# Two-part products in the FFN and column tiles: one wide product for the high weights, halves added at eviction

## What is computed

```python
for l in range(2):                                   # first block
    ...
    hf = rms_norm(x, ffn_norm[l]) @ w_up[l]          # 1024 -> 2 x 2816
    gate, val = hf[..., :2816], hf[..., 2816:]
    gate = depthwise_conv(gate, conv_w[l], conv_b[l])   # 3 taps over the tokens, and a bias
    x = x + (gelu(gate) * val) @ w_down[l]
for l in range(2):                                   # second block
    proj = x @ w_in[l]                               # column part: 10 tiles of 128 channels
    ...
    q = h @ peer_w_q[l]                              # 1024 -> 2048: 16 tiles of 128 channels
    ...
```

## Time and profile before

| | |
|---|---|
| median of three runs | 2944.22 us (2942.88 to 2944.81) |
| the profiled execution | 2944.41 us, its span 2942.6 us |
| instructions in the span | 57193 |
| TensorE busy | 2712.1 us (92%), 17384 matmuls |
| weight loads | 2423.4 us (82%), 17384 |
| VectorE busy | 2088.4 us (71%) |
| ScalarE busy | 1481.8 us (50%) |
| GpSimd busy | 220.9 us (8%) |
| mean granted TensorE clock | 0.961 of full speed |

### The profile page before, as it was taken

One profiled execution on the slowest core, in us unless ns is written; L12 is line 12 of the kernel. 1 busy time (PEld: TensorE's weight loads), 2 busy tenths in 40 slices (PEclk: granted clock), 3 DMA queues, 4 the chain that ended last, 5 costly groups with the idle time before them and its releaser, 6 DMA issues. The chain is left out here.

```text
span 2942.6 us, 57193 instructions
## 1 busy us (share of the span) xinstructions
PE 2712.1 (92%) x17384; PEld 2423.4 (82%) x17384; DVE 2088.4 (71%) x4674; ACT 1481.8 (50%) x2884; POOL 220.9 (8%) x168
## 2 busy tenths in 40 slices
PE   7989989989985899899999999976999899999997
PEld 6759988679874899899988888855999899988886
DVE  5757767567667658977767777676569777777776
ACT  5545555545432445456655555524454466555554
POOL 0000000000020034400000000200144100000000
PEclk9999999999985999999999999977999999999999
DMA  5225553246540557655567777612577555577775
GB/s 190 85 65 172 184 191 101 72 131 184 184 166 1 162 179 229 188 159 174 174 204 233 232 232 233 206 57 79 154 229 215 158 173 176 171 233 234 234 233 180
DMA packets 194020, 504.57 MB, mean 171 GB/s; under 512 B 22528, under 2 KB 88320, under 8 KB 192512
## 3 DMA queue, kind: packets, MB, share of 16 engines
q1 hardware_dynamic: 193920, 503.33, 55.2%
HBM read 468.64 MB, written 34.60 MB: 171 GB/s over the span
## 5 line engine op out<-in xcount | busy, mean ns | idle before, releaser
L182 DVE TENSOR_TENSOR w_lo<-w_raw,w_hi 128x512 fp32r<-128x512 f32 (+2 forms) x1432 | 973.3, 684 | 341.8 <-ACT w_hi L173 321.4
L173 ACT ACTIVATE w_hi<-w_raw 128x512 fp32r<-128x512 f32 (+2 forms) x1592 | 927.1, 621 | 267.4 <-PE banks_right L217 136.8
L215 PE MATMUL up_up<-hT_hi,w_hi 128*128 128x256 f32 x2048 | 594.4, 290 | 26.8 <-DVE w_lo L182 20.7
L217 PE MATMUL up_up<-hT_hi,w_lo 128*128 128x256 f32 x2048 | 581.6, 284 | 0.0
L216 PE MATMUL up_up<-hT_lo,w_hi 128*128 128x256 f32 x2048 | 581.1, 284 | 0.0
L215 PEld LDWEIGHTS up_up<-hT_hi,w_hi 128*128 128x128 f32 x2048 | 394.8, 193 | 31.2 <-DVE w_lo L182 24.0
L227 PE MATMUL banks_left<-w_hi,expert_hi 128*128 128x512 f32 x1024 | 407.6, 398 | 7.8 <-DVE w_lo L182 7.8
L228 PE MATMUL banks_left<-w_lo,expert_hi 128*128 128x512 f32 x1024 | 406.9, 397 | 0.0
L229 PE MATMUL banks_left<-w_hi,expert_lo 128*128 128x512 f32 x1024 | 406.9, 397 | 0.0
L216 PEld LDWEIGHTS up_up<-hT_lo,w_hi 128*128 128x128 f32 x2048 | 394.4, 193 | 0.0
L217 PEld LDWEIGHTS up_up<-hT_hi,w_lo 128*128 128x128 f32 x2048 | 393.7, 192 | 0.0
(11 more groups left out here) (366 smaller groups left out, 4162.3 us busy)
## 6 DMA issues: line engine op xcount, KB each, us to landing
w_raw<-in_peer_u_c SPq DMA_DIRECT2D x256, 512.0 KB, 3.6
w_raw<-in_peer_v SPq DMA_DIRECT2D x256, 512.0 KB, 3.6
w_raw<-in_w_up_c SPq DMA_DIRECT2D x88, 512.0 KB, 3.7
expert_gelu_held<-expert_gelu SPq DMA_DIRECT2D x256, 128.0 KB, 1.8
expert_back<-expert_gelu_held SPq DMA_DIRECT2D x256, 128.0 KB, 3.4
w_raw<-in_w_down SPq DMA_DIRECT2D x44, 512.0 KB, 4.3
w_raw<-in_w_in_r SPq DMA_DIRECT2D x40, 512.0 KB, 3.6
w_raw<-in_w_in_c SPq DMA_DIRECT2D x32, 512.0 KB, 3.7
```

Of the source, the lines that this page charges most:

```text
L173: self.nc.scalar.activation(self.w_hi[:, k % SLOTS, 0:width], self.raw_half(k, width), ACT.Copy).then_inc(self.sem("w_hi_done"), 1)
L182: self.nc.vector.tensor_tensor(self.w_lo[:, k % SLOTS, 0:width], self.raw_half(k, width), self.w_hi[:, k % SLOTS, 0:width].bitcast(F32), A ...
L215: self.nc.tensor.matmul(bank, hi, self.hT_hi[:, c, :], start=(c == 0), stop=False)
L217: last = self.nc.tensor.matmul(bank, lo, self.hT_hi[:, c, :], start=False, stop=(c == DC - 1))
```

## The change

hT_hi and hT_lo become the two halves of one tile, hT, in which the 256 values of the low part follow the 256 of the high part in each chunk. A new `wide_col_half` multiplies w_hi with both in one matmul of 512 columns, which fills a whole PSUM bank: the first 256 values are products with hT_hi, the others with hT_lo. A second matmul adds w_lo with hT_hi to the first 256. The two halves of the bank are added at eviction by VectorE, with a `tensor_reduce` over pairs of values that lie 256 apart. `project` and `gated_loop` use it; the first block's own column tiles and the experts' up products keep `col_half`. In `project` the reduction takes the place of the copy. In `gated_loop` there are two reductions per tile (gate and value) into a new SBUF tile, then a wait for them, and the convolution and the product read that tile instead of PSUM.

```diff
-        self.hT_hi = self.sb("hT_hi", [P, DC, SEQ], F32R)
-        self.hT_lo = self.sb("hT_lo", [P, DC, SEQ], F32R)
+        self.hT = self.sb("hT_hi_lo", [P, DC, 2, SEQ], F32R)
+        self.hT_hi, self.hT_lo = self.hT[:, :, 0, :], self.hT[:, :, 1, :]
...
+    def wide_col_half(self, pe, k, bank, rep=0, entry=None):
+
+        pe.wait_ge(self.sem("w_lo_done"), k + 1 + 2 * SLOTS * rep)
+        for j in range(4):
+            c = 4 * (k % 2) + j
+            if entry is not None:
+                entry.chunk_ready(pe, c)
+            hi = self.w_hi[:, k % SLOTS, j * P:(j + 1) * P]
+            lo = self.w_lo[:, k % SLOTS, j * P:(j + 1) * P]
+            self.nc.tensor.matmul(bank, hi, self.hT[:, c].rearrange("p a n -> p (a n)"), start=(c == 0), stop=False)
+            last = self.nc.tensor.matmul(bank[:, 0:SEQ], lo, self.hT_hi[:, c, :], start=False, stop=(c == DC - 1))
+        last.then_inc(self.sem("w_used"), 1)
...
-                    nc.vector.tensor_copy(cols_dst[:, j, :], col[:, j % 2, 0:SEQ]).then_inc(col_free, 1)
+                    nc.vector.tensor_reduce(cols_dst[:, j, :], col[:, j % 2].rearrange('p (a n) -> p n a', a=2), AX.X,
+                                            ALU.add).then_inc(col_free, 1)
...
-                    K.col_half(pe, k0 + 2 * j + h, col[:, j % 2, 0:SEQ], entry=entry if j == 0 else None)
+                    K.wide_col_half(pe, k0 + 2 * j + h, col[:, j % 2], entry=entry if j == 0 else None)
...
+    both = K.sb(f"{name}_up", [P, 2, n_up, SEQ], F32, ctx)
...
-                nc.scalar.activation(ge[:, b, :], act_in(up, b), ACT.Gelu).then_inc(gelu_done, 1)
+                act.wait_ge(pre_done, j + 1 + unroll * n)
+                nc.scalar.activation(ge[:, b, :], act_in(both, b), ACT.Gelu).then_inc(gelu_done, 1)
...
             def pre(j, n):
-                if gate_dve is not None:
-
-                    dve.wait_ge(used, up_used(j) + 2 * SLOTS * rounds * n)
-                    gate_dve(dve, up, j % 2, j + unroll * n, pre_done)
+                dve.wait_ge(used, up_used(j) + 2 * SLOTS * rounds * n)
+                for q in range(n_up):
+                    nc.vector.tensor_reduce(both[:, j % 2, q, :], up[:, j % 2, q].rearrange("p (a n) -> p n a", a=2), AX.X,
+                                            ALU.add).then_inc(sum_done, 1)
+                dve.wait_ge(sum_done, n_up * (j + unroll * n) + n_up)
+                gate_dve(dve, both, j % 2, j + unroll * n, pre_done)
...
-                nc.vector.tensor_tensor(ac[:, b, :], ge[:, b, :], mult_by(up, b, j + unroll * n),
+                nc.vector.tensor_tensor(ac[:, b, :], ge[:, b, :], mult_by(both, b, j + unroll * n),
...
-                        K.col_half(pe, first + 2 * q + h, up[:, j % 2, q, 0:SEQ], rep=rounds * n,
-                                   entry=entry if q == 0 else None)
+                        K.wide_col_half(pe, first + 2 * q + h, up[:, j % 2, q], rep=rounds * n,
+                                        entry=entry if q == 0 else None)
```

More of the change, by code:

```diff
@@ L612, in gated_loop @@
     used = K.sem("w_used")
-    pre_done, gelu_done, act_done, hi_done, lo_done = (
-        K.sem(f"{name}_{s}_done") for s in ("pre", "gelu", "act", "hi", "lo"))
+    sum_done, pre_done, gelu_done, act_done, hi_done, lo_done = (
+        K.sem(f"{name}_{s}_done") for s in ("sum", "pre", "gelu", "act", "hi", "lo"))
     def at(i):
```

## The result

| | before | after |
|---|---|---|
| median of the runs | 2944.28 us | 2949.18 us (22 runs, 2946.61 to 2952.52) |
| ratio | | 1.0016, interval 1.0009 to 1.0022 |
| profiled execution | 2944.41 us, span 2942.6 | 2949.03 us, span 2947.3 |

The changed kernel is 4.9 us slower. That lies inside the 0.2% that the prediction called "same", and the interval excludes 1: a small loss, not nothing. 2949.2 lies in the range of 2937 to 2992 and 4 us above the 2945.0 forecast, inside that case's own 2939 to 2951. The sum gave +0.1 us; the 4.8 us between them are what the experiments look for. One run of before (9235.83 us) and one of experiment 1 (6757.44 us) lie far outside all others and are left out of ratios and means.

What follows compares the result with a forecast made beforehand. The prediction took TensorE to set the pace; FFN +3.5, query tiles -1.9 and column tiles -1.5 us summed to +0.1 us on 2944.41 us, with 2945 us likeliest after leaning slow, range 2937 to 2992 us (own case 2939 to 2951).

Steps and rivals of the forecast that it cites:

- same: Whole kernel: a time within about 0.2%, 5.9 us, can't be told from no change; chance 0.48.
- Chunk, 0.351 instead of 0.360 us: TensorE: one 512-column and one 256-column product replace three of 256, saving 0.0092 us a chunk, 10.3 us in all.
- Reduction 0.69 us: VectorE: each new reduction of 512 PSUM elements costs as much as the existing contiguous one, 0.69 us.
- strided reading is dear: Rival: VectorE's reductions over values 1 KB apart take 1.18 us instead of 0.69, +44 us, 2989 us; chance 0.18.
- Convolution from SBUF, 0.40 us: VectorE, FFN tile: the first convolution step, reading SBUF instead of PSUM, takes 0.40 us instead of 0.544.
- Stall of 0.13 us, period 8.51: FFN loop: TensorE waits 0.13 us for half 1's low split in every tile; period 8.51 us against 8.53.
- the reductions start where the convolution starts now, 0.45: FFN loop: VectorE begins the reductions 0.45 us after the down tile's first product.
- VectorE is nearly full but doesn't bind.: FFN loop: VectorE keeps up with TensorE, its idle time ahead of this work falling from 0.33 to 0.2 us.
- Edges +1.19 each: First and last FFN tile of each layer: the longer VectorE chain makes TensorE's existing waits 1.19 us longer.
- FFN +3.5 us: Both FFN layers: edges and 20 loop periods at -0.02 us sum to +1.75 us a layer, +3.5 us.
- Query and column tiles, -3.4 us: Query tiles gain 1.9 us and column tiles 1.5 us from shorter products, with evictions mostly hidden.
- within 1.25 us of idle time: Query tiles: the eviction's growth from 0.42 to 0.69 us fits VectorE's 1.25 us idle time per 2.88 us period.

Runs made afterwards that it cites:

- experiment 1: Kernel before with the merged tile, and the wide product with its reduction in query and column tiles only, FFN as before: 2945.82 us, ratio 1.0001.
- Experiment 5: Kernel before with two unused reductions and a wait for them in every FFN tile but each layer's first and last: 2951.43 us, 1.0022.
- 2: Changed kernel with query and column tiles put back to three narrow products and a copy, so only the FFN is changed: 2950.90 us, 1.0015.
- 4: Kernel before with two unused reductions and a wait ahead of the convolution in each layer's first and last FFN tile only: 2955.0 us, 1.0032.
- 6: Changed kernel with the value half's reduction moved behind the convolution, the gate half's still ahead of it: 2948.61 us, 1.0013.
- Experiment 8: Changed kernel with 8 unused products ahead of up tile 1's second half and 10 ahead of the last down tile, per layer: 2944.65 us, 1.0002.
- experiment 9: Kernel before with 3 unused products ahead of up tile 1's second half and 6 ahead of the last down tile: 2944.18 us, 1.0000.
- 7: As 6, with each layer's first FFN tile kept at three narrow products, read from PSUM without a reduction: 2944.75 us, 1.0000.
- 11: As 7, with 3 unused products ahead of up tile 1's second half and 8 ahead of the last down tile: 2942.51 us, 0.9993.
- experiment 10: As 4, with 8 unused products ahead of up tile 1's second half and 10 ahead of the last down tile: 2952.31 us, 1.0026.

## Why the prediction was right, and where it was wrong

- **Chunk, 0.351 instead of 0.360 us.** Right: 0.349. The gain per FFN tile was available in full, 8.53 to 8.38 on TensorE.
- **Reduction 0.69 us.** Right: 0.683 in the FFN, 0.690 in the columns. The "strided reading is dear" rival falls: VectorE reads pairs 1 KB apart in PSUM at the price of a contiguous row (690 ns). The Trainium skill (Advanced Engine Details and Errata, Memory Cachelines) spoke for that rival; the rows here don't bear it out for VectorE's reading.
- **Convolution from SBUF, 0.40 us.** Right: 0.412. Experiment 5, with 0.54 from PSUM, had a period of 8.67.
- **Stall of 0.13 us, period 8.51.** Wrong, and here by the step "the reductions start where the convolution starts now, 0.45". That 0.45 included 0.33 us of idle time; a VectorE without slack comes from a split, finds the bank full, and starts at 0.20. The chain ends 0.25 us sooner, and the stall is gone. The period is 8.42, the loop gives 40 x 0.11 = 4.4 us, not 0.8.
- **"VectorE is nearly full but doesn't bind."** Just wrong: its 8.44 us from reduction to reduction stand against TensorE's 8.38, and the mean period lies between. The idle time of 0.2 us forecast ahead of the reductions isn't there.
- **Edges +1.19 each.** The waits grew by 1.25 and 1.15: right as waits. Wrong as the whole price, and this is the step that matters: "FFN +3.5 us" had only the time that TensorE stood still. It did not ask what the longer standing still does to the clock of the products behind it. A stretch at half clock can follow, ten products and 1.4 to 1.5 us; of eight first-tile waits of 2.08 to 2.19 us in four profiles (changed kernel, 2, 4, 6) four had one. The share of the clock in a single edge is not known better than that.
- **Query and column tiles, -3.4 us.** Wrong: 0.0 (0.65) in experiment 1. The step that failed is "within 1.25 us of idle time": those rows are two ordinary tiles, and the step took them for all 16. Where VectorE also writes the layer norm's output there is no idle time, and 0.7 us a layer are lost again. The trace has +0.5 us for the query tiles, not -1.9, and -1.2 for the column tiles, not -1.5.

The sum again, with what was measured: the FFN's four edges +4.8, their shorter products -0.5, the loop -4.4, columns 0.0, makes -0.1 directly (by the table of layers +0.6 for the FFN, by the trace of experiment 1 -0.7 for the columns: the same). 5.0 of the +4.9 are left over. That remainder is not measured as such. Experiment 8 takes 4.4 (0.8) of it away by keeping TensorE busy, and experiment 9 finds nothing to take away in the kernel before: so most of it is the clock behind the longer waits. An estimate from the granted clocks gives less. The mean over the runs is 0.9586 for the changed kernel and 0.9609 to 0.9615 for the kernel before in the three groups of experiments; from run to run of one kernel 0.001 less goes with about 1.3 us more, which makes 3 to 4 us. But kernels 7 and 11 have 0.959 and are as quick as before, so the mean clock alone doesn't set the time.

The forecast of "no change" was right in name with errors of opposite sign: 3.6 us too little gained in the loop, and 3.4 us (columns) and some 5.0 us (clock) too little lost. That they nearly cancel is luck. The chance of 0.48 for "same" held, but its mechanism, a new stall that eats the loop's gain, isn't what happened.

Open: how the clock's part divides among the four edges (profiles show one slow stretch within the FFN and one just behind it in the changed kernel, three in the FFN-only one, and a profile is one execution); whether the stretch in the attention is more frequent in the changed kernel; why experiment 10 returned less than 8.

## What to carry to other kernels

Work added to an eviction can be hidden in the steady loop and paid in full in the first and last tile, where nothing covers the chain: price those tiles by themselves, and leave the old form there if it is shorter. Idle time read from two tiles need not be there in all: look for tiles in which the engine has other work. A wait on TensorE that grows from about 1 to over 2 us can cost as much again in the products behind it (here behind four of eight), so read the durations of the products after a wait, not only the wait. And look for slow stretches in stages that the change doesn't touch before a difference of two profiled executions is explained. When the start of a step in the old trace has idle time ahead of it, a fuller engine will start it sooner: take off the idle time's part that was only the latency of being woken.

## What was not expected of the hardware

- After waits of 0.84 and 1.54 us the FFN's products of before ran on at 2.4 GHz. After waits of 2.08 to 2.19 us in the first tile ten to fifteen products ran at 1.2 GHz in four of eight cases, in a stretch that began 1.1 to 1.7 us behind the wait's end and lasted 3.2 us in the changed kernel (627.84 to about 631.4): 0.64 us a chunk and not 0.35. With unused products in the gap, which left 0.20 to 0.35 us of waiting, none in the FFN did.
- Such stretches also come where no wait has grown: fourteen products at 818.95 us behind a last tile with the old wait of 1.54 us (experiment 5), and in the attention of a layer in four of the thirteen profiled kernels, 2.4 to 2.5 us each (granted clock 0.77 over 15 us, otherwise 1.00).
- Products that compute nothing needed made the kernel faster: 36 of them, 4.4 us (0.8) in the mean.
- An instruction of VectorE that waits for TensorE in the loop has 0.26 to 0.33 us of idle time in front of it when VectorE stood idle, and none when it came from other work: in the changed loop the reductions follow the split with no idle time and start 0.20 us after the first product of the down tile, where the idle VectorE's started at 0.45.
- VectorE's reduction over two values 1 KB apart in PSUM costs what a contiguous one does, 683 to 690 ns; ScalarE's write at such steps costs 1.09 us against 0.595.
